# Four transformer layers on one core: the start-up order of identity, norm gains, x and first weight quarters

## The reference, cut to what matters

```
def rms_norm(x, g):
    xf = x.astype(jnp.float32)
    y = xf * lax.rsqrt(jnp.mean(xf * xf, axis=-1, keepdims=True) + EPS)
    return (y * g.astype(jnp.float32)).astype(x.dtype)
...
    for l in range(DEPTH):
        h = rms_norm(x, norm1_g[l])
        proj = h @ w_in[l]
```

## Time and profile before

| | us |
|---|---|
| median of 3 runs | 1504.74 |
| lowest and highest | 1504.36, 1505.4 |
| the profiled execution's own time | 1506.56 |
| its span (first to last instruction) | 1504.8 |
| busy: TensorE | 1493.5 |
| busy: VectorE | 1070.4 |
| busy: ScalarE | 800.5 |
| busy: GpSimd | 46.6 |
| memory read, mean rate | 175 GB/s |

### The profile page before, as it was taken

The page is one execution under the profiler, slowest core; times in us unless marked ns, Lnnn a source line. Parts: engine busy times, 40 slices in busy tenths (PEclk is TensorE's granted clock), DMA queues, the critical chain, the costliest instruction groups (busy, mean ns, idle before and its releaser), DMA issues.

```text
span 1504.8 us, 19911 instructions
## 1 busy us (share of the span) xinstructions
PE 1493.5 (99%) x8142; PEld 1273.6 (85%) x8142; DVE 1070.4 (71%) x1357; ACT 800.5 (53%) x958; POOL 46.6 (3%) x52
## 2 busy tenths in 40 slices
PE   9999999999999999999999999999999999999998
PEld 7888888888888888888888888888888888888886
DVE  5778666677786666895757776666877657876666
ACT  5746444466564444666446364444665455454444
POOL 0100000001000000000300100000002100000000
PEclk9999999999999999999999999999999999999999
DMA  8634545554345554445444455554435445455551
GB/s 277 219 132 179 213 179 199 186 192 142 138 171 218 175 196 182 163 175 172 145 165 162 171 193 200 191 195 167 181 125 180 164 166 182 168 212 194 191 197 61
DMA packets 48747, 267.69 MB, mean 178 GB/s; under 512 B 8721, under 2 KB 13201, under 8 KB 18833
## 3 DMA queue, kind: packets, MB, share of 16 engines
q1 hardware_dynamic: 45760, 264.13, 48.6%
q10 hardware_dynamic: 2896, 2.29, 0.5%
HBM read 262.99 MB, written 1.05 MB: 175 GB/s over the span
## 4 chain that ended last, share of the span: by engine, by line
PE 96%; SPq 1%; DMA 1%; ACT 1%; DVE 1%; issue 0%; DVEq 0%; ACTq 0%
PE psum L685 21%; PE psum L589 18%; PE psum L591 18%; PE psum L590 18%; PE psum L694 11%; PE psum L627 4%; DMA raw<-in_weights 1%; PE psum L1005 1%; PE psum L1110 1%; PE psum L858 0%; PE psum L842 0%; PE psum L1024 0%; SPq L519 0%; PE psum L1012 0%; SPq L559 0%; PE psum L1092 0%
## 5 line engine op out<-in xcount | busy, mean ns | idle before, releaser
L1636 DVE TENSOR_TENSOR wl<-raw,wh 128x2048 fp32r<-128x2048 f32 (+1 forms) x247 | 554.7, 2248 | 217.9 <-ACT wh L1211 217.8
L1211 ACT ACTIVATE wh<-raw 128x2048 fp32r<-128x2048 f32 (+2 forms) x249 | 465.8, 1874 | 322.3 <-PE psum L591 195.7
L589 PE MATMUL psum<-wh,xhl 128*128 128x512 f32 (+2 forms) x928 | 365.1, 393 | 1.9 <-ACT work L1245 1.3
L591 PE MATMUL psum<-wh,xhl 128*128 128x512 f32 (+2 forms) x928 | 357.4, 385 | 0.0
L590 PE MATMUL psum<-wl,xhl 128*128 128x512 f32 (+2 forms) x928 | 356.9, 385 | 0.0
L685 PE MATMUL psum<-xhl,wh 128*128 128x512 f32 x1408 | 336.3, 390 | 0.0
L685 PEld LDWEIGHTS psum<-xhl,wh 128*128 128x128 f32 x1408 | 260.9, 188 | 52.1
L589 PEld LDWEIGHTS psum<-wh,xhl 128*128 128x128 f32 x928 | 174.4, 188 | 37.1 <-issue 4.1
L591 PEld LDWEIGHTS psum<-wh,xhl 128*128 128x128 f32 x928 | 174.3, 188 | 34.7
L590 PEld LDWEIGHTS psum<-wl,xhl 128*128 128x128 f32 x928 | 174.6, 188 | 31.6
L694 PEld LDWEIGHTS psum<-xhl,wl 128*128 128x128 f32 x1408 | 175.3, 192 | 3.8
(11 more groups left out here) (209 smaller groups left out, 1172.1 us busy)
## 6 DMA issues: line engine op xcount, KB each, us to landing
raw<-in_weights SPq DMA_DIRECT2D x233, 1024.0 KB, 4.8
raw<-in_weights SPq DMA_DIRECT2D x10, 512.0 KB, 3.6
raw<-in_weights SPq DMA_DIRECT2D x4, 832.0 KB, 4.2
raw<-in_weights SPq DMA_DIRECT2D x12, 256.0 KB, 8.4
raw<-in_weights SPq DMA_DIRECT2D x2, 768.0 KB, 4.0
work<-in_rpb ACTq DMA_DIRECT2D x8, 141.0 KB, 5.7
arena<-arena SPq DMA_DIRECT2D x32, 32.0 KB, 4.3
arena<-work SPq DMA_DIRECT2D x16, 64.0 KB
```

The costliest lines, as they stand in the source:

```text
L589: nc.tensor.matmul(dst, lh, right(wh, slot), start=start, stop=False)
L591: return nc.tensor.matmul(dst, ll, right(wh, slot), start=False, stop=stop)
L1211: nc.scalar.activation(wh[:, slot, 0:n], raw[:, slot, 0:n], ACT.Copy).then_inc(high_ready.sem, 1)
L1636: nc.vector.tensor_tensor(wl[:, slot, 0:n], raw[:, slot, 0:n], wh[:, slot, 0:n].bitcast(F32), ALU.subtract).then_inc(split_ready.sem, 1)
```

## The change

The identity is no longer loaded: GpSimd fills the 128x128 tile with ones and keeps only the diagonal. ScalarE's first transfer is therefore that of the gains. SyncE issues x columns 0 to 511 as one transfer, quarters 0, 1 and 2, x columns 512 to 1023, and the rest as before. TensorE waits for the one transfer ahead of tiles 0 and 1, and transposes tiles 2 and 3 behind the first group of products (kk = 0) instead of ahead of it.

```
-        x_loaded = [ctx.enter_context(nc.semaphore(f"x_loaded_{i}")) for i in range(2)]
+        x_loaded = ctx.enter_context(nc.semaphore("x_loaded"))
...
-        ident_loaded = ctx.enter_context(nc.semaphore("ident_loaded"))
+        ident_filled = ctx.enter_context(nc.semaphore("ident_filled"))
+        ident_ready = ctx.enter_context(nc.semaphore("ident_ready"))
...
-            x_columns(0, 256, x_loaded[0])
-            quarters(0)
-            x_columns(256, 512, x_loaded[1])
-            quarters(1, 2)
+            x_columns(0, 512, x_loaded)
+            quarters(0, 1)
+            quarters(2)
             x_columns(512, 1024, x_rest_loaded)
...
-            pe.wait_ge(ident_loaded, 16)
+            pe.wait_ge(ident_ready, 1)
...
                 def x_second():
-                    pe.wait_ge(x_loaded[1], 16)
                     pe.sem_inc(x_ready.sem, 2)
                     tiles_t((2, 3))
...
                 if layer == 0:
-                    pe.wait_ge(x_loaded[0], 16)
+                    pe.wait_ge(x_loaded, 16)
                     tiles_t((0, 1))
                     nc.tensor.matmul(bank(PROJ)[:, 0:SEQ], xf[:, 0, 0:P], xf[:, 0, 0:SEQ], start=True, stop=True)
-                    x_second()
-                    first_piece(0, {2: x_rest})
+                    first_piece(0, {0: x_second, 2: x_rest})
...
         def _(act):
-            act.dma_start(ident[:, :], consts["ident"]).then_inc(ident_loaded, 16)
             act.dma_start(gain1[:, :, :], gains1).then_inc(gain1_loaded, 16)
...
         def _(pool):
+            nc.gpsimd.memset(ident[:, :], 1.0).then_inc(ident_filled, 1)
+            pool.wait_ge(ident_filled, 1)
+            nc.gpsimd.affine_select(out=ident[:, :], in_=ident[:, :], compare_op=ALU.is_equal, fill=0.0, base=0,
+                                    pattern=[[1, P]], channel_multiplier=-1).then_inc(ident_ready, 1)
             pool.wait_ge(consts_loaded, 16 * len(loads))
```

## The result

| | before | changed |
|---|---|---|
| median of 22 executions each, us | 1505.85 | 1508.07 |
| lowest to highest | 1504.36 to 1507.58 | 1507.34 to 1510.22 |
| span of the profiled execution | 1504.8 | 1506.1 |
| its own time | 1506.56 | 1507.88 |

A forecast was written before the change was run, and what follows sets the result against it. TensorE, busy 1493.5 of 1504.8 us, bounds the kernel; its resume at 45.33, set by ScalarE's run, sets the end. A delay of +0.8 on the median 1504.74 gives 1505.5, range 1504.0 to 1507.3.

The forecast's parts named there:

- Identity, gains, x in two transfers: Kernel start: identity ready by about 2 us, gains landing at 5.9, first x transfer at 5.4, later transfers issued 0.5 earlier.
- S = 8.1: Moment of TensorE's first product, 8.13 before; forecast 8.1, kept between 7.3 and 8.7 us.
- the latest landing of x: First x transfer landing at 6.8 us, which would put the first product at 8.6.
- The moved transposes: Tiles 2 and 3 behind the first six products: new 0.65 us wait ahead of the third group, tile 4's copy at 14.1.
- The later of 45.33 + d and 44.02 + e: Where TensorE resumes after its 1.3 us wait near 45; the kernel's end was to move one for one with it.
- d: Delay of ScalarE's run, taken at tile 4's copy after 13.28; forecast +0.8 us, the amount put into the sum.
- e: Delay of TensorE's own arrival at the wait near 45, before at 44.02; forecast +1.4 us, arriving at 45.4.
- The clock: Rival: TensorE idles ahead of the first products, so they run at half pace and the kernel is slower; chance 0.25.
- its first form: Clock rival with only the first group at half pace: tile 4's copy some 1.0 us later, 1506.5 us; chance 0.21.
- The long form: Clock rival with half pace through three groups: tile 4 late by 3.2 on top of 0.8, about 1508.5 us; chance 0.04.
- The gap is about 1 us: Argument against the clock rival: TensorE's new idle time from the warming products' end until x lands is only about 1 us.
- The remark that I cited on transposes: Transposes don't count as busy like products, so moving them would not matter to the clock; weighed under the clock rival.

The follow-up runs named there:

- ident_alone: The kernel before with the identity made by GpSimd and without ScalarE's identity transfer; median 1505.37 us, ratio to before 0.9999.
- filled: The changed kernel with more warming products on TensorE, ahead of x and behind the first transposes; median 1505.99 us, ratio to before 1.0003.
- filled_back: filled with the transposes of tiles 2 and 3 back ahead of the first products; median 1504.87 us, ratio to before 0.9995.
- filled_q2: filled with quarter 2 ahead of tiles 2 and 3 in ScalarE's and VectorE's order; median 1505.12 us, ratio to before 0.9996.
- piece7_first: The kernel before with weight piece 7 issued ahead of the twelve mask transfers and second gains; median 1505.58 us, ratio to before 0.9999.
- order_back: The changed kernel with the transposes of tiles 2 and 3 back ahead of the first products; median 1505.50 us, ratio to before 1.0002.
- order_alone: The kernel before with only the transposes of tiles 2 and 3 moved behind the first products; median 1506.77 us, ratio to before 1.0009.
- before_filled: The kernel before with two more 128-column warming products, behind the first and the second transposes; median 1505.45 us, ratio to before 0.9997.
- change_again: The changed kernel run once more as it is, on another chip; median 1508.01 us, ratio to before 1.0017.

## Why the prediction was wrong, point by point

- **Identity, gains, x in two transfers: no loss.** None that can be told from nothing (0.9999 and 1.0002). The select took 0.29 us, under my 0.6. x landed at 5.6 against 5.4. I had feared that the gains' 192-byte pieces hold x up. In ident_alone, where they went first, x's first 256 KB took 3.3 us against 3.1. The Trainium skill (DMA: Bandwidth & Descriptors, Specifications) says that a DMA engine reads, modifies and writes for pieces under 512 bytes. No run here shows whether it does so.
- **Start of the products, S = 8.1.** Right as a number: 8.16. It was quarter 0, at 6.7, that set it. By quarter 0 I had 7.7 to 8.0, and 8.1 was a pick between that and the latest landing of x.
- **The moved transposes: a wait of 0.65, tile 4 at 14.1, TensorE 1.4 later.** Right where the clock is up: 0.56, 14.08, and filled stands 1.4 behind filled_back by their spans (1504.3 and 1502.9). filled_q2 shows the mechanism.
- **"The later of 45.33 + d and 44.02 + e".** This step failed for the median. I took 1.3 us of the delay as swallowed by a wait that one execution showed, and put d = 0.8 into the sum instead of my e = 1.4. Between the two profiles of before and changed the wait did swallow 1.3 us; but only 3 of the 13 profiles with that order of issues have it, so it can't be counted on. The order costs 1.1 us by the medians of filled and filled_back, 1.4 by their spans, which is e and not d.
- **The clock.** The main failure. The sum put it at nothing. I had it as a rival at 0.25, with the right place, sign and evidence (the gap from 4.48, the group at 6.96 gone), and priced it at 1.0 us for its first form. It came in both profiles of the changed kernel. Its price by the runs is some 2.1 us. The first group and the four transposes behind it took 11.51 - 8.16 = 3.35 us against 1.87 in filled, so 1.5 us went there (1.2 in the six products, where I had 1.5 at most, and 0.3 in the transposes), and tile 4 was 1.5 later, not 1.0. I had priced six products and then let part of it be absorbed by a wait that in fact stayed at 0.55. Where the rest of the 2.1 us lies stays open. The long form's 1508.5 is near the measured 1508.07 by luck: half pace did not last through three groups in either profile.
- **"The gap is about 1 us"** was what I held against it. The two gaps were 1.2 and 1.4 us, and the second stood directly ahead of the products.
- **The Trainium skill on the clock.** The Trainium skill (TensorE: Matmul & The Clock Gate, What's actually happening) says that the same kernel may show different numbers of slow matmuls at its start. The traces agree: the kernel before and piece7_first, alike up to there, ran the first group at 0.23 and at 0.43. I should have drawn from it that one profile with a fast start is no evidence of a fast start. The remark that I cited on transposes, that they don't count as busy in the way products do (the Trainium skill, TensorE: Matmul & The Clock Gate, Part 4: PE-mode transpose), is not settled. order_back and the changed kernel differ in the place of four transposes alone; full pace came at 9.86 where they filled the gap, and at 11.5 and 13.1 where they didn't. That speaks against it, but it is one execution against two.

The change taken apart by the runs: clock 2.2 us (1.0018 against 1.0003), order 1.2 (1.0003 against 0.9995), and 0.7 less in filled_back than in the kernel before. These add up to the ratio's 2.7 us by the way they are formed, so the sum is no check of them. TensorE's positions in the profiles give 1.6, 1.5 and 0.4 for the same three, in single executions. Ratios to the kernel before carry an uncertainty near 1.4 us each, and the 0.7 can't be told from nothing; between the filled kernels and the changed one the executions don't overlap.

**Open:** why order_alone's executions reach 1509.56, why before_filled still spreads over 2 us, what stretches SyncE's run of small issues in some executions, and which of the two gaps does more.

## What to carry to other kernels

When a reorder moves TensorE work out of an idle stretch, cost the stretch it leaves empty as well as the place where it goes: here the idle stretches ahead of the first product (one from the moved transposes, one from x's later landing) cost about twice what the new wait did, and a few products on zeros bought it back. Behind a moved producer, look at what stands in the same engine's queue and doesn't need it (quarter 2's split behind tile 2's copy). And don't let a wait seen in one execution absorb a delay before asking whether the median of many executions contains that wait.

## What the runs showed that I had not expected

- The granted clock's column is not enough at the start of a kernel. In order_back it reads 1.00 while products are 0.43 apart, so the durations have to be read too:

```profile
8.50:9.00 0.50, 0.50 (x1) 0.41 (x2) 0.50 (x2) 0.50 (x3) 0.00 (x0) 1.00 1.04 401
...
9.00 0.63 PE L590 MATMUL psum<-wl,xhl 128*128 128x512 f32 x1
9.43 0.63 PE L591 MATMUL psum<-wh,xhl 128*128 128x512 f32 x1
```

- SyncE's run of small issues from piece 5 to piece 7, the same instructions each time, took 14.85 us in the kernel before, 14.44 in the changed one and 12.64 in filled_back. It doesn't follow the change: change_again, the same kernel as the changed one, has 12.80. The difference lies in single issues: that of the 128 KB table is one. In the kernel before and in filled_back:

```profile
24.01 1.75 SPq L519 DMA_DIRECT2D rope_b<-in_table_rope_b  x1
```

```profile
23.46 0.45 SPq L520 DMA_DIRECT2D rope_b<-in_table_rope_b  x1
```

- The kernels with both gaps covered are also the steadier ones: filled_back's 11 executions lie within 0.54 us, filled_q2's within 0.68, filled's within 1.22; the kernel before's 33 on the chip of filled_back and filled lie within 4.1. That the covered gaps are the reason is not shown, since order_back, which has a gap ahead of x, lies within 1.41 and before_filled within 1.95.
